# Reordering VectorE's merge and factor sums, one TensorE join and one GpSimd wait at the end of a hybrid attention decode step

## The reference, cut to what matters

```python
o_b = jnp.einsum('bqhc,chv->bqhv', o_lat, w_kv_up[..., MLA_NOPE:]).reshape(b, t, MLA_WIDTH)
pa = (o_a * jax.nn.silu(ga)) @ w_proj_a
pb = (o_b * jax.nn.silu(gb)) @ w_proj_b
h = jax.nn.sigmoid(ma) * pa + jax.nn.sigmoid(mb) * pb
return x + _rmsnorm(h @ w_out, norm_post)
```

## Time and profile before

| what | value |
|---|---|
| median of 3 runs (lowest, highest) | 679.22 us (677.92, 679.77) |
| the profiled execution's own time, and its span | 677.92 us, 676.1 us |
| TensorE busy | 650.7 us, 96% of the span |
| VectorE busy | 447.2 us, 66% |
| ScalarE, GpSimd busy | 215.2 us (32%), 72.0 us (11%) |
| granted TensorE clock, mean | 0.998 of full speed |

### The profile page before, as it was taken

The page is one execution under the profiler, slowest core; times in us unless marked ns, Lnnn a source line. Parts: engine busy times, 40 slices in busy tenths (PEclk is TensorE's granted clock), DMA queues, the critical chain, the costliest instruction groups (busy, mean ns, idle before and its releaser), DMA issues.

```text
span 676.1 us, 15338 instructions
## 1 busy us (share of the span) xinstructions
PE 650.7 (96%) x5771; PEld 432.4 (64%) x5771; DVE 447.2 (66%) x1232; ACT 215.2 (32%) x586; POOL 72.0 (11%) x75
## 2 busy tenths in 40 slices
PE   8999999999999988899999998999999999999995
PEld 3444444553576755577678685678788888886443
DVE  2198799686587767756665673647486656648865
ACT  0311322677444444444453542331011111110221
POOL 0344343130000000210202000000000000000011
PEclk9999999999999999999999999999999999999999
DMA  8999999997699999978849689929521102018011
GB/s 332 413 422 424 424 426 397 364 368 218 225 357 391 387 399 413 409 255 308 313 166 344 235 270 402 407 77 369 230 85 63 63 23 102 1 66 340 3 63 62
DMA packets 67443, 179.44 MB, mean 265 GB/s; under 512 B 7497, under 2 KB 16226, under 8 KB 60074
## 3 DMA queue, kind: packets, MB, share of 16 engines
q1 hardware_dynamic: 56456, 125.67, 50.5%
q0 software_dynamic: 8128, 48.38, 17.5%
q10 hardware_dynamic: 2786, 4.42, 1.8%
HBM read 169.38 MB, written 12.72 MB: 269 GB/s over the span
## 4 chain that ended last, share of the span: by engine, by line
PE 82%; DVE 5%; DMA 5%; SPq 2%; ACT 2%; issue 2%; another core or an unknown queue 0%; DVEq 0%; ACTq 0%
PE bank L1527 20%; PE bank L946 12%; PE bank L1366 8%; PE bank L1578 7%; PE bank L1227 5%; PE bank L1350 4%; PE bank L1335 3%; PE bank L1253 3%; PE bank L1237 3%; DMA projP<-x 3%; PE bank L1556 2%; PE bank L1110 2%; PE bank L1300 1%; DMA ring<-win 1%; PE bank L1310 1%
## 5 line engine op out<-in xcount | busy, mean ns | idle before, releaser
L946 PE MATMUL bank<-W,XG 128*128 128x494 f32 x192 | 83.6, 580 | 0.8 <-DVE projP L1957 0.8
L1834 ACT ACTIVATE projP<-bank,projP 128x128 f32<-128x128 f32 (+3 forms) x96 | 49.9, 525 | 41.3 <-DVE projP L2313 40.2
L2613 DVE TENSOR_TENSOR projP<-projP,bank 128x260 f32<-128x260 f32 x81 | 32.6, 423 | 42.3 <-PE bank L1527 41.6
L1366 PE MATMUL bank<-W 128*128 128x260 f32 x256 | 60.4, 389 | 0.0
L1627 ACT ACTIVATE projP<-bank 128x128 f32<-128x128 f32 (+5 forms) x87 | 33.8, 392 | 82.5 <-PE bank L1527 47.7
L946 PEld LDWEIGHTS bank<-W,XG 128*128 128x128 f32 x192 | 35.2, 192 | 36.6 <-issue 35.0
L1366 PEld LDWEIGHTS bank<-W 128*128 128x128 f32 x256 | 47.3, 190 | 10.8 <-issue 3.7
L1627 ACT ACTIVATE W<-bank 128x512 f32<-128x512 f32 (+2 forms) x69 | 40.1, 583 | 43.3 <-PE bank L989 11.3
L2313 DVE CUSTOM_DVE_ANT_0 bank<-bank,maskb 128x128 f32<-128x128 f32 (+3 forms) x96 | 45.8, 511 | 12.2 <-PE bank L1227 10.1
L1227 PE MATMUL bank<-W 64*128 64x128 f32 (+7 forms) x192 | 46.0, 466 | 0.5 <-ACT projP L1834 0.4
L788 POOL DMA_INDIRECT ring<-cmp,idxi x32 | 38.6, 1206 | 68.0 <-DVE VV L2024 47.9
(11 more groups left out here) (472 smaller groups left out, 1165.0 us busy)
## 6 DMA issues: line engine op xcount, KB each, us to landing
ring<-latent SPq DMA_DIRECT2D x176, 256.0 KB, 4.4
XG<-latent SPq DMA_DIRECT2D x64, 256.0 KB
W<-w_gate SPq DMA_DIRECT2D x12, 1024.0 KB, 5.9
W<-w_attn SPq DMA_DIRECT2D x16, 494.0 KB, 11.9
rope_rows<-ring SPq DMA_DIRECT2D x16, 256.0 KB, 7.0
KRR<-rope_rows ACTq DMA_DIRECT2D x16, 256.0 KB
ring<-win SPq DMA_DIRECT2D x8, 512.0 KB, 6.8
ring<-w_out SPq DMA_DIRECT2D x2, 2048.0 KB, 11.7
```

What stands on the lines that cost most here:

```text
L946: mm = pe.matmul(bank[2 * (u % 2) + n][:, 0:GW], XG[:, k * TOK + tl * P:k * TOK + (tl + 1) * P], w_part(half, k, n), start=(k == 0), stop= ...
L1366: mm = pe.matmul(bank[6][:, 0:HALF], gate_w[g % 2][:, at:at + P], X2[:, k * TOK + hf * HALF:k * TOK + (hf + 1) * HALF], start=(k == 0), st ...
L1834: act.activation(Pb[u % 4][:, 0:w], bank[u % 2][:, 0:w], ACT.Exp, bias=NMp[:, u:u + 1], scale=-1.0, accum_out=RSp[:, u:u + 1]).then_inc(S[ ...
L2613: dve.tensor_tensor(out, a, pair_bank(v, product)[:, 0:HALF], ALU.add).then_inc(S["z_by_dve"], 1)
```

## The change

On TensorE, join "obd" comes after product 5 of ma (p3) instead of product 4 (p2), counted from 0. On GpSimd, the two last multiplications no longer wait for the reciprocal root of tile 1. On VectorE, four steps change places: `gate_sums(0)` goes ahead of `join("parts")`; the p2 and p3 additions of ma go ahead of `join("obd")` and `output_sums("pb")` (this matters in round 0 alone); those of pa go ahead of `gate_sums(1)` in round 0; and the addition of the partial mean for tile 3 goes from before row half (1, 0) to after row half (1, 1). No instruction is added or taken away, except the two waits on GpSimd.

```diff
--- before.py
+++ after.py
@@ -440,7 +440,7 @@
         LAST_HALVES = ((0, 1), (2, 0), (1, 1), (3, 0))
         ROWS_DONE = (TILES, 0, 2, 1, 3)
         JOINS = ("parts", "coef", "lat", "turn", "obd")
-        JOIN_AFTER = {(0, 1): "parts", (1, 1): "coef", (2, 1): "lat", (2, 3): "turn", (2, 4): "obd"}
+        JOIN_AFTER = {(0, 1): "parts", (1, 1): "coef", (2, 1): "lat", (2, 3): "turn", (2, 5): "obd"}
         GATE_JOBS = [("gb", 0), ("gb", 1), ("ga", 0), ("ga", 1)] + [(kind, q) for q in range(4) for kind in ("mb", "ma")]
         GATE_AT = {"ga": 0, "gb": 2, "ma": 4, "mb": 8}
         ztiles = tail
@@ -844,7 +844,6 @@
             for part, added in enumerate((out_added["c21a", 1], out_added["c21", 1])):
                 lo = part * 256
                 pool.wait_ge(S["z_by_dve"], added)
-                pool.wait_ge(S["inv_root"], ROWS_DONE.index(1) + 3)
                 pool.tensor_tensor(normed[:, 1536 + lo:1792 + lo], H[:, 3 * D_MODEL + lo:3 * D_MODEL + lo + 256],
                                    OB[:, lo:lo + 256], ALU.mult).then_inc(S["normed"], 1)
 
@@ -2660,8 +2659,8 @@
 
             merge()
             input_sums()
+            gate_sums(0)
             join("parts")
-            gate_sums(0)
             join("coef")
             for q in range(4):
                 mb, ma, pb, pa = (tile_no[kind, 2 * q] for kind in ("mb", "ma", "pb", "pa"))
@@ -2681,10 +2680,10 @@
                 proj_sums("pa", q)
                 if 0 < q < 3:
                     gate_sums(2 * q + 1)
+                add_p2_p3(ma)
                 if q == 0:
                     join("obd")
                     output_sums("pb")
-                add_p2_p3(ma)
                 add_p4(ma)
                 add_p6(pb)
                 if q == 0:
@@ -2699,9 +2698,9 @@
                     dve.tensor_tensor(out_s("s3"), h11, h21, ALU.subtract).then_inc(S["o_sums"], 1)
                 add_p6(pa)
                 add_p5_p7(pa)
+                add_p2_p3(pa)
                 if q == 0:
                     gate_sums(1)
-                add_p2_p3(pa)
                 add_p4(pa)
                 gate_outputs(pa)
 
@@ -2817,11 +2816,11 @@
                     finish(2, 0)
             rows_added("c21a", 1, rows(3, 0), rows(3, 0), "p4", 0, 256)
             root_of(1, 1)
-            dve.wait_ge(S["sqz"], SQUARES.index((3, 0, "a")) + 1)
-            dve.tensor_tensor(vfirst[:, 3:4], vfirst[:, 3:4], ssz[:, 10:11], ALU.add).then_inc(S["mean_sq"], 1)
             out_half(1, 0)
             rows_added("c21", 1, rows(3, 0), rows(3, 0), "p4", 256, 512)
             out_half(1, 1)
+            dve.wait_ge(S["sqz"], SQUARES.index((3, 0, "a")) + 1)
+            dve.tensor_tensor(vfirst[:, 3:4], vfirst[:, 3:4], ssz[:, 10:11], ALU.add).then_inc(S["mean_sq"], 1)
             root_of(3, 0)
             out_half(3, 0)
             out_half(3, 1)
```

## The result

The changed kernel took 683.54 us (median of 8 runs, 681.14 to 685.14), the kernel before on the same chip 678.6 us (8 runs, 677.15 to 680.68). The ratio is 1.0069, 95% interval 1.0052 to 1.0088: 4.7 us slower (0.0069 x 678.6), between 3.5 and 6.0. The medians are 4.9 us apart. The forecast was slower by 3.35 us. The profiled execution took 682.35 us, with a span of 680.5 us and a mean granted clock of 0.992, against 677.92, 676.1 and 0.998 before. Lines after the one taken away are numbered one less: L1447 after is L1448 before.

What follows compares the result with a forecast made beforehand. TensorE was taken to bound the merge, VectorE the end after 667 us. Delays of 1.9 + 0.4 + 0.75 + 0.3 = 3.35 us on the 679.22 us median gave 682.6 us, range 680.3 to 684.2.

Steps and rivals of the forecast that it cites:

- Edit 1: gate_sums(0) ahead of join("parts"): VectorE stands for late gate weights, so TensorE waits 1.9 us for the coefficients.
- Edit 2: join "obd" after p3, ma's additions ahead of it: TensorE waits at p6 of pb, 0.4 us in all.
- Edit 3: pa's p2 and p3 additions ahead of gate_sums(1): TensorE waits 0.75 us at p6 of mb.
- Edit 4: The end: GpSimd's removed wait gains 0.2 us, but the later partial mean delays the last reciprocal; 0.3 us later.
- A: Rival at the gate weights: they land in time, gate_sums(0) ahead costs nothing, 1.45 us left, 680.7 us; chance 0.15.
- B: Rival at p4 of pb: VectorE's queue is relieved, TensorE's gaps go, -0.8 us; 679.5 or 678.6 us; chance 0.05.
- C: Rival at all four places: worse waits of 2.9, 0.8, 1.1 and 0.9 us, 5.7 in all, 684.9 us; chance 0.07.
- D: Rival: nothing to be seen, all four signals still come before they are wanted, 679.2 us; chance 0.03.

Runs made afterwards that it cites:

- the first comparison: The changed kernel's first runs against the kernel before: 683.54 against 678.6 us, ratio 1.0069 (1.0052 to 1.0088).
- the second: The changed kernel run once more, unaltered, against the kernel before on the same chip: ratio 1.0058 (1.0040 to 1.0076).
- sums_early: Kernel before with output_sums("pa") ahead of add_p6(pb) on VectorE and without GpSimd's wait, against the kernel before: ratio 0.9985 (0.9972 to 0.9999).

## Why the prediction was right, and where its sizes were off

The four delays came at the places forecast, for the reasons given, and their steps in the table make 3.5 us (1.75, then 0.54 and 0.06, then 0.88, then 0.31) against 3.35. That the time of 683.54 us lies in the range of 680.3 to 684.2 us owes something to luck: the forecast started from 679.22 us, the median of three runs, and eight gave 678.6. From there the same range ends at 683.6, and the measured time would be only just inside.

- **Edit 1, the wait.** Forecast 1.9 us, measured 1.75 and, alone, 1.89 in the bracket. The landing (471.31, 11.6 us after its issue), the join behind it and the idle TensorE came as worked out, except that the 0.10 us put in for the coefficients' signal was 0.06 (477.10 to 477.16), and the loads reordered showed the cause. One reason given for it was wrong: the copy issued behind the load has no part in it, only what is ahead.
- **Edit 1, the clock.** This term was missing from the sum: it priced the wait, not what the wait may do to the work after it. In the profiled execution it was 1.67 us. On average it is open: filling the wait gave back 1.0 us with an error of 0.5. The four delays alone (3.5 us) stand at the lower end of the interval of the first comparison (3.5 to 6.0 us) and well inside that of the second (2.7 to 5.2), so that the times do not prove the term; it is the likeliest reason for what the first comparison (4.7) has above them. The Trainium skill ("TensorE: Matmul & The Clock Gate", "What's actually happening") says that TensorE's clock passes either all or half of its pulses, by how busy it has been. The windows agree with the two levels (0.50 and 1.00). By that rule an added wait can cost clock, and the forecast had no such rival; here the fall came behind the wait in one of four profiled executions.
- **Edit 2, "obd".** Forecast 0.4 us, measured 0.6 (0.54 and 0.06). The mechanism was right, that the two waits are one and the same delay. What was left out is the way from the end of the sums to the first matmul: 496.61 + 0.70 = 497.31 to 497.46, 0.15 us. The bound of 0.8, that the two waits add up, did not come true.
- **Edit 3.** Forecast 0.75 us, measured 0.88, alone too. Here also the 0.15 us from 512.12 to 512.27 is what was missing.
- **Edit 4.** Forecast 0.3 us, measured 0.31, with each step as worked out: "c21a" to "c21" 2.14 us (forecast 2.13), the reciprocal 2.09 us behind "c21" (forecast 2.11). Apart, the two edits give -0.13 and +0.03, so that they cost 0.4 us more together than one by one, in one execution of each. The moved addition alone lets VectorE come first at row half (1, 0), and the removed wait puts GpSimd first again, at the root.
- **The rivals.** A (weights in time) did not happen, and the loads reordered gave about its time: 1.0016 is 1.1 us, where it had 1.45. B's gap is real, but the changed kernel does not close it: sums_early does, in another way. C did not happen as a mechanism: its delays of 2.9, 0.8, 1.1 and 0.9 us came as 1.75, 0.6, 0.88 and 0.31, though in sum the 4.7 us of the first comparison are nearer to its 5.7 than to 3.35. D did not happen.

## What to carry to other kernels

When the order on a helper engine is changed, ask of each instruction that moves ahead what it waits for: an instruction that waits for a transfer holds all that is behind it, however short it is itself. A wait put on a busy TensorE may also cost clock behind it: 1.67 us behind 1.75 in one profiled execution, nothing in three others. And an idle stretch just ahead of a busy one on the helper engine is the place to put work which the bound engine needs soon.

## What the runs showed of the hardware

- The granted clock fell to 0.50 only 1.4 us after TensorE had begun to work again, behind a wait of 1.68 us by the bracket, and stayed there for 3.4 us of dense matmuls; behind waits of 1.75, 1.77 and 1.89 us at the same place in three other executions it did not fall.
- A 1 MB load queued behind 4 MB landed 11.6 us after its issue, and 4.7 us after it when it was issued ahead of them. With the 4 MB copy behind it taken away the landing was the same (11.7 us); there the DMA engines' share was 0.13 and 0.08 from 469.0 to 470.5, and the landing came 0.7 us later.
- Behind a wait of 2.1 to 3.5 us for a load, at about 249 us in these executions, the granted clock fell to 0.50 for 3.4 us in 7 of 14; in the other seven, waits of 1.7 to 3.1 us at this place were passed at 1.00. In two of the 14 it fell for as long at 135 us, with no wait ahead.
- VectorE and GpSimd stood for each other in both directions: 0.64 us instead of 0.22 for a one-column VectorE operation that came 0.1 us after GpSimd's, and 1.23 us instead of 0.72 for a GpSimd part that VectorE preceded by 0.11 us. The Trainium skill ("SBUF — State Buffer", "Who interferes with whom") says that the one which starts first keeps the shared ports for its whole instruction; both cases here agree.
